# Output projection of the delta layer in seven half-size products per 512 columns, first half of the tokens first

## The reference, cut to what matters

```
def gated_deltanet_layer(h, in_w, conv_w, A_log, dt_bias, onorm_g, out_w):
    ...
    o = chunk_gated_delta_rule(q, k, v.astype(jnp.float32), g, beta)
    o = rmsnorm_2(o, onorm_g) * jax.nn.silu(z.astype(jnp.float32))
    return o.astype(h.dtype).reshape(Bn, T, A_WIDTH) @ out_w      # the product that is changed

    # in second_block, for each layer l
    h = rmsnorm_2(x, norm_g[l]) * (1.0 + scale) + shift           # for l = 1: the norm behind it
    ...
    x = x + gate * out
    if l == N_A_LAYERS - 1:
        shared = nsa_shared_kv(x, kv_norm_g, kv_w, ...)
```

## Time and profile before

| what | value |
|---|---|
| runs of the kernel before | 1178.71, 1179.72, 1181.79 us; median 1179.72 |
| span of the profiled execution | 1177.4 us, 2.3 below that median |
| TensorE busy (PE) | 1164.3 us, 99% of the span |
| VectorE busy (DVE) | 737.2 us, 63% |
| ScalarE busy (ACT) | 352.1 us, 30% |
| GpSimd busy (POOL) | 86.2 us, 7% |
| mean granted TensorE clock | 0.997 of full |
| DMA | 241.78 MB, 205 GB/s on average |

### The profile page before, as it was taken

How to read it: one execution, slowest core, us unless ns; L and a number is a source line. 1 busy time by engine, 2 the same in 40 slices (tenths; PEclk the granted TensorE clock), 3 DMA queues, 4 the chain that set the end, 5 groups by cost and what they waited for, 6 DMA issues and landing times.

```text
span 1177.4 us, 21319 instructions
## 1 busy us (share of the span) xinstructions
PE 1164.3 (99%) x8862; PEld 1076.8 (91%) x8862; DVE 737.2 (63%) x1658; ACT 352.1 (30%) x996; POOL 86.2 (7%) x104
## 2 busy tenths in 40 slices
PE   9999999999999999999999999999999999999997
PEld 7889999998878999999999999988888998888887
DVE  4558888675148866982898888567845231167632
ACT  2111210232124555212321210245333431056542
POOL 0000000200011000022000000310004010001111
PEclk9999999999999999999999999999999999999999
DMA  9969949762655457676599759574524643642311
GB/s 344 366 217 321 315 154 313 290 245 90 219 180 187 150 214 259 236 264 231 185 342 304 235 201 294 193 260 171 146 61 144 215 144 114 187 136 73 117 63 36
DMA packets 164272, 241.78 MB, mean 205 GB/s; under 512 B 14033, under 2 KB 112559, under 8 KB 164176
## 3 DMA queue, kind: packets, MB, share of 16 engines
q1 hardware_dynamic: 156256, 230.45, 57.9%
q10 hardware_dynamic: 6784, 5.74, 1.7%
q0 software_dynamic: 1136, 4.22, 1.1%
HBM read 236.82 MB, written 4.62 MB: 205 GB/s over the span
## 4 chain that ended last, share of the span: by engine, by line
PE 91%; DVE 5%; DMA 2%; ACT 1%; issue 1%; POOL 0%; DVEq 0%; ACTq 0%
PE ps L189 89%; PE ps L192 2%; DVE arena L198 2%; DMA slots<-in_w_proj_a 1%; DVE x L198 1%; DMA slots<-in_w_proj_b 1%; ACT U L195 1%; DVE slots L207 1%; ACT tmps L195 0%; DVE arena L204 0%; DVE rstd L216 0%; DVE tmps L204 0%; DVE slots L198 0%; DVE tmps L198 0%; POOL arena L198 0%
## 5 line engine op out<-in xcount | busy, mean ns | idle before, releaser
L189 PE MATMUL ps<-U,slots 128*128 128x128 f32 (+2 forms) x2800 | 478.7, 330 | 0.0
L189 PEld LDWEIGHTS ps<-U,slots 128*128 128x128 f32 (+1 forms) x2800 | 419.7, 190 | 40.7 <-issue 4.7
L189 PE MATMUL ps<-arena,slots 128*128 128x128 f32 (+1 forms) x1776 | 237.6, 294 | 0.0
L189 PEld LDWEIGHTS ps<-arena,slots 128*128 128x128 f32 x1776 | 225.3, 192 | 8.6 <-issue 0.4
L195 ACT ACTIVATE tmps<-ps 128x256 f32<-128x256 f32 (+2 forms) x151 | 57.4, 383 | 343.4 <-PE ps L189 319.4
L207 DVE CUSTOM_DVE_ANT_0 arena<-arena,tmpA 128x1024 f32<-128x1024 f32 x96 | 118.2, 1275 | 19.3 <-DMA arena<-in_w_adaT 19.1
L195 ACT ACTIVATE arena<-ps 128x256 f32<-128x256 f32 (+3 forms) x150 | 59.5, 416 | 155.9 <-PE ps L189 152.1
L189 PE MATMUL ps<-arena 128*128 128x128 f32 (+7 forms) x940 | 101.9, 287 | 0.9 <-DVE arena L198 0.9
L189 PEld LDWEIGHTS ps<-arena 128*128 128x128 f32 (+2 forms) x940 | 92.4, 181 | 9.8 <-issue 4.2
L189 PE MATMUL ps<-ABT,arena 128*128 128x128 f32 (+5 forms) x752 | 81.9, 271 | 0.0
L189 PEld LDWEIGHTS ps<-ABT,arena 128*128 128x128 f32 (+3 forms) x752 | 72.5, 174 | 0.8 <-issue 0.8
(11 more groups left out here) (199 smaller groups left out, 1140.6 us busy)
## 6 DMA issues: line engine op xcount, KB each, us to landing
slots<-in_w_in SPq DMA_DIRECT2D x14, 2048.0 KB, 10.3
slots<-in_w_down SPq DMA_DIRECT2D x16, 1408.0 KB, 9.8
slots<-in_w_gate SPq DMA_DIRECT2D x18, 1024.0 KB, 8.0
slots<-in_w_up SPq DMA_DIRECT2D x18, 1024.0 KB, 10.8
arena<-in_w_adaT SPq DMA_DIRECT2D x36, 512.0 KB, 6.1
arena<-in_ada_w1T SPq DMA_DIRECT2D x24, 512.0 KB, 7.5
slots<-in_a_in_w SPq DMA_DIRECT2D x6, 2048.0 KB, 9.8
slots<-in_b_in_w SPq DMA_DIRECT2D x12, 1024.0 KB, 5.4
```

Source lines behind the costliest of these rows:

```text
L189: return Nothing() if self.e is None else self.e.matmul(*a, **k)
```

## The change

The columns of a 512-column block (a unit `u`, 0 or 1) are taken as two pairs of 128-column blocks (m = 0, 1; in a pair j = 0, 1), the 1024 inputs as two halves (g = 0, 1) of four chunks, the tokens as two halves. With W[g, j] for a quarter of the weights, and a11, a12 (a21, a22) for the two input halves of the first (second) half of the tokens, seven products stand for eight:

- weights: t1 = W01 - W00, t2 = W11 - t1, t3 = W11 - W01, t4 = W10 - t2; t1 and t2 go to `x7` (unit 0) or to a free part of `arena` (unit 1), t3 and t4 replace W01 and W10 in the slot
- tokens: S1 = a21 + a22, S2 = S1 - a11, S3 = a11 - a21, S4 = a12 - S2 (`v_s7`, now also for `OG`)
- bank A (for unit 1 a pair of banks, 6 and 7): p1 = W00 a11, then p6 = t2 S2, p7 = t3 S3 and p4 = t4 a22 are added to it; ScalarE copies it out after p1 (s1), after p6 (u2) and after p7 (u3)
- bank C (for unit 1 banks 4 and 5): p2 = W10 a12 in one part; p5 = t1 S1 and then p3 = W11 S4 in the other; ScalarE copies p5 out (s5)
- first half of the tokens: s1 + p2 for j = 0, u2 + p5 + p3 for j = 1; second half: u3 + s5 for j = 1, and bank A after p4 for j = 0

Each part is added to `H` by VectorE with the gate as it comes (`h7_add`, always 128x128). TensorE's order runs both units side by side: p1, p1, p2, p2, p5, p5, p6, p6, p3, p3, p7, p7, p4, p4, each 16 instructions in the trace, with the sums of the first half in the middle of the second p7. On VectorE the first three weight differences of unit 0 are put ahead of `v_do(e, 0)`, those of unit 1 behind the third gate block. `late("n5")` becomes 0: all four pairs of chunks are squared and added per half. The sums of this norm get bank 5 (`R5`) instead of a turn in the ring `X`. The slots of `ao` are closed after p4 of their unit.

The diff, cut (left out are the short functions for addresses, products p5 to p4, ScalarE's other copies, and lines where the ring's name alone changes):

```diff
         TB = ring(*[tmpB[:, i, :] for i in range(3)])
         TC = ring(*[tmpC[:, i, :] for i in range(3)])
 
+        R5 = ring(banks[5][:, :])
+        SUMS = {"n5": R5}
         S3 = ring(*[b[:, :] for b in banks[3:6]])
         X2 = ring(*[b[:, :] for b in banks[6:8]])
...
+            return {"n1": 4, "n2": 3, "n3": 2, "n4": 3, "n5": 0, "no": 2}[tag]
+
+        def sums_ring(tag):
+
+            return SUMS.get(tag, X)
 
         def s_square(e, tag, c2, half=None):
 
...
         def p_squares(e, tag):
 
+            if late(tag) == 0:
+                for half in range(2):
+                    acc, sq = sq_acc(tag, "sq")[:, HALF[half]], TC.buf("sq", tag, 0, half)
+                    e.wait_ge(*act.at("sq", tag, 0, half))
+                    e.tensor_tensor(acc, sq[:, 0:P], sq[:, P:T], ALU.add).then_inc(*pool.up())
+                    TC.close([pool.now()], "sq", tag, 0, half)
+                    for c2 in range(1, 4):
+                        p_squares_late(e, tag, "sq", c2, half)
+                return
             for c2 in range(1, late(tag)):
...
+        HE = ring(*[tmpB[:, i, :] for i in range(3)])
+        RA1, RC1 = ring(psum[:, 6:8, :]), ring(psum[:, 4:6, :])
+        H7_T = {"ao": [(x7[:, 0:1024], x7[:, 1024:2048]), (arena[:, 4096:5120], arena[:, 5120:6144])]}
+        H7_GAIN = {"ao": mods[:, 88:96]}
+        H7_BANKS = {"ao": L}
...
+        def t_h7(e, n, p, u, out, weights, tokens, start=False, amid=None):
+            for m in range(2):
+                if m and amid:
+                    amid(e)
+                for k in range(4):
+                    i = e.matmul(out[:, m, :], weights[:, k, m, :], tokens[:, k, :], start=start and k == 0 and (u == 1 or m == 0), stop=k == 3, skip_group_check=True)
+                i.then_inc(*pe.up(n, p, u, m))
+        def t_h7_p1(e, n, u, src, ready):
+            _, free = h7_ring(n, "A", u).open(n, "A", u)
+            for x in free:
+                e.wait_ge(*x)
+            e.wait_ge(*arrived(n, u))
+            for k in range(4):
+                e.wait_ge(*ready(k, 0))
+            t_h7(e, n, "p1", u, h7_banks(n, u)[0], w_h7(n, u, 0, 0), src[:, 0:4, HALF[0]], True)
+        def t_h7_p2(e, n, u, src, ready):
+            _, free = h7_ring(n, "C", u).open(n, "C", u)
+            for x in free:
+                e.wait_ge(*x)
+            for k in range(4, 8):
+                e.wait_ge(*ready(k, 0))
+            t_h7(e, n, "p2", u, h7_banks(n, u)[1][:, :, 0, :], w_h7(n, u, 1, 0), src[:, 4:8, HALF[0]], True)
...
+        def t_h7_units(e, n, src, ready, tag, first_a, first_c):
+            def sums(e):
+                for x in free_of(RC1):
+                    e.wait_ge(*x)
+                t_sums_half(e, tag, 0)
+            t_h7_p1(e, n, 0, src, ready)
+            for x in first_a:
+                e.wait_ge(*x)
+            t_h7_p1(e, n, 1, src, ready)
+            t_h7_p2(e, n, 0, src, ready)
+            for x in first_c:
+                e.wait_ge(*x)
+            t_h7_p2(e, n, 1, src, ready)
+            for u in range(2):
+                t_h7_p5(e, n, u)
+            for u in range(2):
+                t_h7_p6(e, n, u)
+            for u in range(2):
+                t_h7_p3(e, n, u)
+            t_h7_p7(e, n, 0)
+            t_h7_p7(e, n, 1, amid=sums)
+            for u in range(2):
+                t_h7_p4(e, n, u, src)
+        def s_h7_s1(e, n, u):
+            _, free = HE.open(n, "e", u)
+            for x in free:
+                e.wait_ge(*x)
+            e.wait_ge(*pe.at(n, "p1", u, 1))
+            e.activation(h7_first_sums(n, u)[:, 0], h7_banks(n, u)[0], ACT.Copy).then_inc(*act.up(n, "s1", u))
...
+        def s_h7_units(e, n, tag, first):
+            for x in first:
+                e.wait_ge(*x)
+            for u in range(2):
+                s_h7_s1(e, n, u)
+            s_squares_early(e, tag)
+            for u in range(2):
+                s_h7_s5(e, n, u)
+            for u in range(2):
+                s_h7_u2(e, n, u)
+            for c2 in range(4):
+                s_square(e, tag, c2, 0)
+            s_h7_u3(e, n, 0)
+            s_root(e, tag, 0, squares=False)
+            s_h7_u3(e, n, 1)
+        def v_h7_t12(e, n, u):
+            e.wait_ge(*arrived(n, u))
+            e.tensor_tensor(t_of_h7(n, u, 0), w_h7(n, u, 0, 1), w_h7(n, u, 0, 0), ALU.subtract).then_inc(*dve.up(n, "t1", u))
+            e.wait_ge(*dve.at(n, "t1", u))
+            e.tensor_tensor(t_of_h7(n, u, 1), w_h7(n, u, 1, 1), t_of_h7(n, u, 0), ALU.subtract).then_inc(*dve.up(n, "t2", u))
+        def v_h7_t3(e, n, u):
+            e.wait_ge(*dve.at(n, "t1", u))
+            e.tensor_tensor(w_h7(n, u, 0, 1), w_h7(n, u, 1, 1), w_h7(n, u, 0, 1), ALU.subtract).then_inc(*dve.up(n, "t3", u))
+        def v_h7_t4(e, n, u):
+            e.wait_ge(*pe.at(n, "p2", u, 1))
+            e.wait_ge(*dve.at(n, "t2", u))
+            e.tensor_tensor(w_h7(n, u, 1, 0), w_h7(n, u, 1, 0), t_of_h7(n, u, 1), ALU.subtract).then_inc(*dve.up(n, "t4", u))
+        def h7_add(e, n, c, half, x):
+            h = H[:, c, HALF[half]]
+            return e.stt(h, x, H7_GAIN[n][:, c:c + 1], h, ALU.mult, ALU.add)
+        def v_h7_early(e, n, u, ready):
+            for i, name in enumerate(("s1", "u2")):
+                for m in range(2):
+                    c = 4 * u + 2 * m + i
+                    e.wait_ge(*ready(c))
+                    e.wait_ge(*act.at(n, name, u))
+                    h7_add(e, n, c, 0, h7_first_sums(n, u)[:, i, m, :]).then_inc(*dve.up(n, name, u, m))
+        def v_h7_half0(e, n, u):
+            C2 = h7_banks(n, u)[1]
+            for m in range(2):
+                for j in range(2):
+                    e.wait_ge(*dve.at(n, ("s1", "u2")[j], u, m))
+                    e.wait_ge(*pe.at(n, "p3", u, h7_read(u, m)))
+                    h7_add(e, n, 4 * u + 2 * m + j, 0, C2[:, m, j, :]).then_inc(*dve.up("res", n, 4 * u + 2 * m + j, 0))
+            h7_ring(n, "C", u).close([dve.now()], n, "C", u)
+        def v_h7_s5(e, n, u):
+            for m in range(2):
+                e.wait_ge(*act.at(n, "s5", u))
+                h7_add(e, n, 4 * u + 2 * m + 1, 1, h7_fifth(n, u)[:, m, :]).then_inc(*dve.up(n, "fifth", u, m))
+            if u:
+                HE.close([dve.now()], n, "s5")
+        def v_h7_u3(e, n, u):
+            for m in range(2):
+                e.wait_ge(*dve.at(n, "fifth", u, m))
+                e.wait_ge(*act.at(n, "u3", u))
+                h7_add(e, n, 4 * u + 2 * m + 1, 1, h7_first_sums(n, u)[:, 0, m, :]).then_inc(*dve.up("res", n, 4 * u + 2 * m + 1, 1))
+            HE.close([dve.now()], n, "e", u)
+        def v_h7_last(e, n, u):
+            A = h7_banks(n, u)[0]
+            for m in range(2):
+                e.wait_ge(*pe.at(n, "p4", u, h7_read(u, m)))
+                h7_add(e, n, 4 * u + 2 * m, 1, A[:, m, :]).then_inc(*dve.up("res", n, 4 * u + 2 * m, 1))
+            h7_ring(n, "A", u).close([dve.now()], n, "A", u)
+        def v_h7_units(e, n, tag, ready, scale):
+            for u in range(2):
+                v_h7_t4(e, n, u)
+            for u in range(2):
+                v_h7_early(e, n, u, ready)
+            v_h7_half0(e, n, 0)
+            for u in range(2):
+                v_h7_s5(e, n, u)
+            v_h7_half0(e, n, 1)
+            scale()
+            v_h7_u3(e, n, 0)
+            v_root(e, tag, 0)
+            v_normed(e, tag, 0)
+            v_h7_u3(e, n, 1)
+            for u in range(2):
+                v_h7_last(e, n, u)
+            v_root(e, tag, 1)
+            v_normed(e, tag, 1)
...
             for g in range(4):
                 t_on_turn(e, g)
             og = lambda k, half: dve.at("og", k // 2)
-            for pair in range(4):
-                t_linear(e, "ao", pair, OG, og, half=0 if pair >= 2 else None)
-            for x in free_of(OO):
-                e.wait_ge(*x)
-            t_linear(e, "ao", 2, OG, og, half=1)
-            t_sums_half(e, "n5", 0)
-            t_linear(e, "ao", 3, OG, og, half=1)
+            t_h7_units(e, "ao", OG, og, "n5", free_of(DO, 0) + free_of(OO, 3), free_of(OO, 1, 2))
             t_linear(e, "nq", 0, U, u_in("n5"), half=0, side=True)
             t_sums_half(e, "n5", 1)
             t_linear(e, "nq", 1, U, u_in("n5"), half=0)
@@ -3676,11 +3921,17 @@
             v_dc_silus(e, 11)
             v_q_columns(e)
             v_silu(e, "zg", 1, ZG[:, 2:4, :])
+            v_h7_t12(e, "ao", 0)
+            v_h7_t3(e, "ao", 0)
             v_do(e, 0)
             v_d_queries(e, 2)
             v_do(e, 1)
             v_d_queries(e, 3)
             v_silu(e, "zg", 2, ZG[:, 4:6, :])
+            for x in (pe.at("d v", g) for g in range(4)):
+                e.wait_ge(*x)
+            v_h7_t12(e, "ao", 1)
+            v_h7_t3(e, "ao", 1)
             v_on_mean(e)
             v_on_rstd(e)
             v_on_scale(e, 0)
@@ -3689,15 +3940,8 @@
                 if g == 3:
                     v_silu(e, "zg", 3, ZG[:, 6:8, :])
                 v_og(e, g)
```

(16 more changed lines are left out.)

63 lines of the change are left out of this document (57 added, 6 removed).

## The result

| | kernel before | changed kernel |
|---|---|---|
| median of the runs, taken together | 1180.91 us (12 runs) | 1183.60 us (12 runs) |
| span of the profiled execution | 1177.4 us | 1182.4 us |
| TensorE busy | 1164.3 us | 1165.4 us |
| VectorE busy | 737.2 us | 753.5 us |

The ratio is 1.0020, with a 95% interval of 1.0012 to 1.0028: slower, by less than the 0.3% that the prediction took as the smallest change that can be told. The forecast was 1183.0. It was near by luck, and not for the reasons that it gave: two of its terms were too large, and one wait was not foreseen at all.

The account below looks back on a forecast made before the run. It took TensorE's work as the bound, with the norm's chain close by. 2.3 (v_do(0) wait) plus 1.05 (later second sums) made 3.35 us on 1177.4, 1180.75; the median's 2.3 above the span gave 1183.0, range 1179.8 to 1186.0.

Parts of the forecast that it names:

- wait ahead of the solving step: TensorE waits near 904 for v_do(0), delayed by unit 0's t1 to t3: 2.3 us, bounds 0.55 to 2.6.
- The turns of t1 to t3: Ahead of v_do(0), unit 0's differences alternate with GpSimd's multiplications; t2 and t3 each come 1.88 to 2.05 us later.
- at their normal pace: Without turns, unit 0's t1 to t3 let v_do(0) end at 904.5, and TensorE loses 0.55 us.
- its own sign: Prediction is wrong if differences keep 1.22 us beside a busy GpSimd, or the first sums come without a wait.
- The place of the first sums: In the projection, first-half sums stand at 951.3, only 0.5 us earlier than before, with TensorE idle 2.7 us ahead.
- Sums to sums: From first-half to second-half sums 9.45 us instead of 7.9, with TensorE idle 1.1 us before the second.
- Behind the second sums: TensorE runs on into the B layer, so a shift of the second sums reaches the end whole.
- TensorE's work: The projection takes 224 instructions, 25.0 us instead of 28.1: a gain of 3.1 us at most.
- What moves besides: Fetches of cmp_k, near 954.6 instead of 941.27, and b_in are covered; ScalarE's eight copies fall in idle time.
- The clock: Rival: TensorE's clock falls in the wait of 2.3 or 2.7 us; one drop 1185, two 1187; chance 0.08.
- the likeliest case: Forecast's own case: turns with GpSimd and late sums, slower by 3.35 us, 1183.0 us; chance 0.70.
- turns in one place alone: VectorE and GpSimd alternate at only one of two places, 1180.6 to 1181.4 us; listed under no turns, chance 0.12.

Follow-up runs that it names:

- e8_beside_add: Changed kernel with the first unit's t1 to t3 one step later, between the third group's d queries and v_do(1), beside GpSimd's additions; 1186.87 us, single run.
- e3_two_in: Changed kernel with GpSimd's eight multiplications of H taking g_final as a second tensor operand instead of one factor per partition; 1184.55 us, ratio 1.0037.
- e4_s5_last: Changed kernel with the fifth product's four additions behind the second unit's first-half columns instead of ahead of them; 1182.51 us, ratio 1.0014.
- e7_four: Changed kernel with the unused L turn, late t1 to t3, late fifth-product additions, and second-half squares among the first half's scalings; 1178.80 us, ratio 0.9986.
- e1_turn: Changed kernel with one unused turn of ring L, so later users keep their banks from before the change; 1182.37 us, ratio 1.0010.
- e5_before_turn: Kernel before with two unused turns of ring L behind the output projection, giving later users the changed kernel's banks; 1182.85 us, ratio 1.0016.

## Why the prediction was right, and where it was not

The number came within 0.6 us of the median, and the range and the sign held. Its sum was 3.35 us and the trace gives 2.42; term by term:

| term | predicted | measured | how |
|---|---|---|---|
| wait ahead of the solving step | +2.3 | +0.71 | 910.87 - 902.23, against 907.58 - 899.65 |
| first sums, without that wait | -0.5 | -1.24 | 51.61 - 52.14 - 0.71 |
| first to second sums | +1.55 | +1.43 | 9.33 - 7.90 |
| behind the second sums | 0 | +1.52 | 280.17 - 60.94, against 277.75 - 60.04 |

That the number came near is luck. The terms miss by -1.59, -0.74, -0.12 and +1.52 us, and the wait that was not foreseen makes up for most of what the others had too much. The time hides a second offset: the forecast stood on a median of three runs (1179.72) that lies 1.19 us below that of twelve (1180.91), and its rise of 3.35 us was 0.66 above the 2.69 of the medians.

- **The turns of t1 to t3: the step that failed.** I took GpSimd's stream to be one kind of neighbour, and gave its multiplications the turns that the earlier trace rows show beside additions. The trace has 0.45 of wait and 0.26 more behind it, near the bound of 0.55 "at their normal pace". By its own sign ("wrong if the differences keep 1.22 beside a busy GpSimd") the prediction was wrong here: they kept 1.21 to 1.38. e8_beside_add has the forecast turns beside additions, and e3_two_in has turns beside the same multiplications written with a second tensor operand. The forecast that GpSimd's multiplications would be lengthened was right (2.26 us), but I took it as a sign that both pay. The Trainium skill, SBUF — State Buffer, "Who interferes with whom", which I had weighed as the rule against this place, says that a VectorE instruction with two SBUF inputs and a reading GpSimd instruction shut each other out for a whole instruction. e8_beside_add agrees (1.94 to 2.21 us apart); beside the one-input multiplications the measurement differs (1.25 and 1.31), and decides.
- **The place of the first sums: the right mechanism, mis-sized.** GpSimd does lengthen the fifth product's additions, and e4_s5_last shows that these four hold the first sums (1.05 us earlier without them in front), but what GpSimd adds to them is 0.69 us (1.83 - 1.14) and not the 1.25 that I took (0.42 for each of three GpSimd additions). TensorE's idle time there was 1.80 instead of 2.7.
- **Sums to sums: right.** 9.33 against 9.45; the wait 0.83 against 1.1. The extra square and its additions are what I said, and e7_four shows that ScalarE's order is the lever.
- **Behind the second sums: the step that was missing.** I let a shift run through to the end and looked behind the sums only at the queue of weights. That the projection opens a ring four times less, and so moves each later user to another bank, stands in the diff; I had not followed it. e1_turn and e5_before_turn show that it costs 1.5 us here.
- **TensorE's work: right.** From 931.00 to the end of the row at 955.03 there are 224 instructions. From the projection's start to the second sums, less the waits shown, TensorE takes 29.54 us (963.17 - 931.00 - 1.80 - 0.83) against 32.07 (959.69 - 927.26 - 0.36): 2.5 of the 3.1 us, the rest in restarts and in the wait for og 3 that the forecast had put at 929.73. The saving is there, and the waits eat it. One of them the forecast had not: from the gate to the projection's start it is 28.77 us (931.00 - 902.23) against 27.61 (927.26 - 899.65), which is the 0.71 and 0.45 more. The new first product waits until the heads of all its four chunks are gated (the 0.28 at 931.00), where `t_linear` waited for one chunk at a time. It is a part of the -1.24 above, and no run takes it away.
- **What moves besides: right.** The fetch of in_cmp_k_w, 16 us later in the execution, is covered; the second unit's t1 to t3 and the token differences are hidden.
- **The clock: right that it would stay.** It was at 1.00 in the stretches of the projection, with a wait of 1.80 us. The 3.24 us of e8_beside_add brought it down, and the price that I gave the rival, 2 us for a drop, was of the right size (3.39 - 1.76 = 1.63). The longest wait that left it at 1.00 is one of 1.96 us (e5_before_turn, at 479.27), so what the 2.3 or 2.7 us of the forecast would have done to it is not shown.

So the likeliest case was not the one that happened. Of the cases listed, "turns in one place alone", priced 1180.6 to 1181.4 (its terms give 1181.3 either way, 0.55 + 1.05 or 2.3 - 0.7), is what the trace shows up to the second sums, with 0.90 us (60.94 - 60.04), at its lower end; the wait that I had missed added 1.5 us. The 0.69 us fits the turns of the experiments: there VectorE lost GpSimd's own pace less 0.15 to 0.27 us a turn (1.07 and 0.96 of 1.23, 0.42 and 0.30 of 0.57); for additions of 128x128, one every 0.41 us at best, that makes 0.14 to 0.26, and three of them at 948.90 to 949.95 cost 0.23 each (0.69 / 3). That is an estimate, tested by no run. What stays open: why the multiplications with one tensor input take no turn from VectorE, and why the four products of one row at the program's start take up to 1.75 us longer in some executions.

## What to carry to other kernels

A change that opens a ring of buffers more or fewer times moves every later user of that ring: count the opens modulo its size, and look at each place that names a buffer by its number. Beside GpSimd ask which form its instructions have, as additions of two tensors cost VectorE up to 1.1 us a difference here, short multiplications of two tensors up to 0.4, and multiplications by a factor per partition 0.17 in all. And a saving on the busiest engine is worth having only once the chain beside it has been shortened as well: here some 2.5 us less of TensorE's work became a gain of 1.6 us only after four repairs: the turn of L, the place of t1 to t3, that of the fifth product's additions and that of the second half's squares.

## What the hardware showed that I had not expected

- GpSimd's multiplications with one tensor input gave way to VectorE's differences: 9.51 instead of 7.25 us for the eight, while three differences of 128x1024 kept 1.21 to 1.38. With a second tensor operand at the same place and in the same order (e3_two_in) VectorE paid as well, 1.37 to 1.63, and beside additions of 128x512 (e8_beside_add) 1.91 to 2.28. GpSimd lost 0.98 us a turn in both; VectorE lost 0.66 us a turn more beside the instruction that by itself takes 0.66 us longer. The Trainium skill, SBUF — State Buffer, "Who interferes with whom", says that the order of issue and not the shape decides who is blocked; here the place in both lists and the 128x256 shape were the same and the form made the difference.
- TensorE's granted clock stayed at 1.00 through waits of 1.47, 1.80 and 1.96 us and fell behind one of 3.24 us (0.60 on the mean of the 4 us from 916), at a cost of 1.63 us on the next twelve instructions. One execution shows the fall.
